# Feed-forward by seven block products for eight, in two phases, with half of the weight sums on GpSimd

## The reference

```
def swiglu_ffn(hn, w_gate, w_up, w_down):
    return (jax.nn.silu(hn @ w_gate) * (hn @ w_up)) @ w_down

h = h + swiglu_ffn(rms_norm(h, norm_ffn_w[l]), w_ffn_gate[l], w_ffn_up[l], w_ffn_down[l])
h = rms_norm(h, norm_final_w)
return h[:, N_META:]
```

## Time and profile before

| | |
|---|---|
| median of 3 runs | 2921.02 us (2920.89 to 2921.11) |
| span of the profiled execution | 2921.4 us |
| the profiled execution's own time | no figure apart from its span, which is 0.4 us above the median |
| PE busy | 2891.1 us, 14928 matmuls |
| DVE, ACT, POOL busy | 1146.6, 760.4, 354.5 us |
| moved | 280.75 MB, 96 GB/s on average |

### The profile page before, as it was taken

One profiled execution on the slowest core, in us unless ns is written; L12 is line 12 of the kernel. 1 busy time (PEld: TensorE's weight loads), 2 busy tenths in 40 slices (PEclk: granted clock), 3 DMA queues, 4 the chain that ended last, 5 costly groups with the idle time before them and its releaser, 6 DMA issues.

```text
span 2921.4 us, 38375 instructions
## 1 busy us (share of the span) xinstructions
PE 2891.1 (99%) x14928; PEld 2449.9 (84%) x14928; DVE 1146.6 (39%) x1436; ACT 760.4 (26%) x929; POOL 354.5 (12%) x358
## 2 busy tenths in 40 slices
PE   8999999999999999999999999999999999999998
PEld 8999888888889878888888888888888888888887
DVE  4444555555452344422432323333332323233334
ACT  4443322222222322222322222222222222222222
POOL 5000244433334201100200000000000000000000
PEclk9999999999999999999999999999999999999999
DMA  4333222222223324433133333232323233232322
GB/s 142 87 87 93 73 80 80 79 79 79 85 80 108 94 82 148 151 123 122 58 101 96 96 97 95 94 94 94 94 94 95 96 97 95 94 94 94 94 94 108
DMA packets 234900, 280.75 MB, mean 96 GB/s; under 512 B 10777, under 2 KB 192162, under 8 KB 234146
## 3 DMA queue, kind: packets, MB, share of 16 engines
q1 hardware_dynamic: 230450, 270.91, 29.7%
q10 hardware_dynamic: 4352, 8.39, 0.8%
HBM read 266.68 MB, written 12.58 MB: 96 GB/s over the span
## 4 chain that ended last, share of the span: by engine, by line
PE 97%; DVE 1%; ACT 1%; issue 1%; POOL 1%; DMA 0%; SPq 0%; DVEq 0%; POOLq 0%; ACTq 0%
PE psum L1395 66%; PE psum L1421 7%; PE psum L1420 7%; PE psum L1419 7%; PE psum L1577 2%; PE psum L1372 1%; PE psum L1572 1%; PE psum L1347 1%; PE psum L1556 0%; PE psum L1650 0%; POOL hn_lo L475 0%; PE psum L1534 0%; ACT f_junk L913 0%; PE psum L1550 0%; PE psum L1547 0%
## 5 line engine op out<-in xcount | busy, mean ns | idle before, releaser
L923 DVE TENSOR_TENSOR w_lo<-w_raw,w_hi 128x1024 fp32r<-128x1024 f32 x472 | 589.9, 1250 | 1301.9 <-ACT w_hi L653 1300.3
L1395 PE MATMUL psum<-hn_lo,w_hi 128*128 128x512 f32 (+1 forms) x2976 | 997.8, 361 | 0.0
L1395 PE MATMUL psum<-hn_hi,w_lo 128*128 128x512 f32 (+1 forms) x2976 | 994.4, 360 | 0.0
L1395 PE MATMUL psum<-hn_hi,w_hi 128*128 128x512 f32 (+1 forms) x2976 | 993.1, 360 | 0.0
L653 ACT ACTIVATE w_hi<-w_raw 128x1024 fp32r<-128x1024 f32 x472 | 499.5, 1058 | 1540.4 <-PE psum L1395 945.2
L1395 PEld LDWEIGHTS psum<-hn_hi,w_hi 128*128 128x128 f32 x2976 | 528.8, 188 | 85.1 <-issue 0.2
L1395 PEld LDWEIGHTS psum<-hn_lo,w_hi 128*128 128x128 f32 x2976 | 527.8, 188 | 84.3 <-issue 0.7
L1395 PEld LDWEIGHTS psum<-hn_hi,w_lo 128*128 128x128 f32 x2976 | 528.5, 188 | 81.3
L1420 PE MATMUL psum<-w_lo,a_hi 128*128 128x512 f32 x672 | 265.8, 396 | 0.0
L1421 PE MATMUL psum<-w_hi,a_lo 128*128 128x512 f32 x672 | 265.8, 395 | 0.0
L1419 PE MATMUL psum<-w_hi,a_hi 128*128 128x512 f32 x672 | 265.7, 395 | 0.0
(11 more groups left out here) (280 smaller groups left out, 2277.5 us busy)
## 6 DMA issues: line engine op xcount, KB each, us to landing
w_raw<-in_w_in SPq DMA_DIRECT2D x144, 512.0 KB, 3.6
w_raw<-in_w_ffn_gate SPq DMA_DIRECT2D x88, 512.0 KB, 3.5
w_raw<-in_w_ffn_up SPq DMA_DIRECT2D x88, 512.0 KB, 3.5
w_raw<-in_w_ffn_down SPq DMA_DIRECT2D x88, 512.0 KB, 3.7
w_raw<-in_w_out SPq DMA_DIRECT2D x32, 512.0 KB, 3.7
gates_dram<-gate_out ACTq DMA_DIRECT2D x16, 512.0 KB, 2.8
w_raw<-in_w_proj_a SPq DMA_DIRECT2D x16, 512.0 KB, 6.5
w_raw<-in_w_proj_b SPq DMA_DIRECT2D x16, 512.0 KB, 8.2
```

Of the source, the lines that this page charges most:

```text
L923: dve.tensor_tensor(wlo[s][:], raw[s][:], whi[s][:].bitcast(F32), ALU.subtract).then_inc(S["lo_ready"], 1)
L1395: ins = pe.matmul(o, lhs, r, start=kt == 0 and i == 0, stop=kt == 4 * n_chunks - 1 and i == 2)
```

## The change

The feed-forward is cut into blocks, and each 2x2 block product is formed with seven products of blocks instead of eight (Winograd's form of Strassen's scheme): some blocks are added first, and the results are combined with more additions. It is done in two phases: first gate and up for all 5632 hidden columns, with the activations written to a DRAM tensor, then down.

Gate and up. A unit is 256 columns of gate or of up: 22 pairs of units. The weights of a unit (2048x256, `fraw`, two buffers) are four blocks: upper and lower half of the rows, left and right 128 columns. The token side is split once, ahead: seven combinations of y = the normalised h (`s_hi`, `s_lo`), each 1024 rows by 256 tokens. A product is 24 matmuls over 256 columns. Per unit:
- VectorE forms two sums of weight blocks in one instruction (`t_pair`, `t13`: two times 1024 elements).
- GpSimd forms the other two (`sums`: `t2`, and then in place in `fraw`), 1024 elements each, the second after the first.
- ScalarE writes the high parts in four instructions (`hi_a`, `hi_2`, `hi_b`, `hi_c`: 2048, 1024, 2048, 2048 elements), VectorE the low parts (`low_a`, `low_2`, `low_b`, `low_c`). None of these buffers is doubled.
- Banks of PSUM are read in the middle of the sums: three copies on ScalarE (`e0`, `e1`, `e0`) and three additions on VectorE (C11, C22, C12; `c_done`).

Per pair ScalarE applies silu, VectorE multiplies and forms four sums (`up_products`), the seven results of 256 tokens (`comb`) are split and stored to DRAM by two transfers that ScalarE issues (`comb_store`, 0.92 MB each).

Down runs in twelve steps of 512 plus 512 columns: for each block of hidden rows (2, 4, 4, 4, 4, 4 times 256) two steps. Per step SyncE loads four blocks of weights, VectorE forms four sums of them (`dn_sum`), ScalarE and VectorE split seven blocks, and VectorE adds each of the seven products from PSUM to `hq`, which holds h in quarters (`dn_read`, 1024 elements). h is stored to DRAM during the output projection and read back as `hq`; y is written over h. Every second step the activations of the next block are loaded. The final norm comes after the last of these.

The core of the diff, with the instructions that the prediction speaks of:

```diff
-            gate_up(G_FFN, 0)
-            with sp.Fori(0, N_FFN // 2) as i:
-                g = G_FFN + 16 + 48 * i
-                gate_up(g, 2 * i + 1)
-                down(g + 16, 2 * i)
-                gate_up(g + 24, 2 * i + 2)
-                down(g + 40, 2 * i + 1)
-            down(G_END - 8, N_FFN - 1)
+            sp.wait_ge(S["lo_ready"], G_FFN)
+            ffn_load(0, 0)
+            sp.wait_ge(S["h1_ready"], FREE["h1_ready"] + TT * N_OUT)
+            store_h(N_OUT - 1)
+            sp.wait_ge(S["s_sum"], 4)
+            sp.wait_ge(S["x_lo"], X0 // 2 + 4)
+            ffn_load(0, 1)
+            with sp.Fori(1, PAIRS) as j:
+                for g in range(2):
+                    sp.wait_ge(S["lo_ready"], half_of(2 * j + g - 1, 3))
+                    ffn_load(j, g)
...
+            sp.wait_ge(S["comb_stored"], 32 * KAPPA[0])
+            for q, what in enumerate(ORDER):
+                sp.wait_ge(S["chunk_used"], USED0 + 7 * (UNITS - 1) + min(q // 2 + 1, 4))
+                act_load(0, what)
+            sp.wait_ge(S["chunk_used"], USED0 + 7 * UNITS - 2)
+            hq_load(0)
...
+            def sums(j, g):
+
+                n = 2 * j + g
+                pool.wait_ge(S["t_done"], n + 1)
+                after(pool, "chunk_used", 7 * n - 4, USED0)
+                pool.tensor_tensor(t2[:], t13[:, 0, :, :], fraw[g][:, HEADS:KT, P:UNIT], ALU.add).then_inc(S["t_pool"], 1)
+                pool.wait_ge(S["t_pool"], 2 * n + 1)
+                pool.tensor_tensor(fraw[g][:, 0:HEADS, P:UNIT], t2[:], fraw[g][:, HEADS:KT, 0:P], ALU.add) \
+                    .then_inc(S["t_pool"], 1)
...
+            def unit_act(j, g, last=False, beside=lambda: None):
+
+                n = 2 * j + g
+                act.wait_ge(S["chunk_used"], USED0 + 7 * n + 1)
+                after(act, "c_done", 3 * (n) - 1)
+                act.activation(e0[:], PS[:, 3 * g, 0:UNIT], ACT.Copy).then_inc(S["evicted"], 1)
+                split_c(n, g)
+                act.wait_ge(S["chunk_used"], USED0 + 7 * n + 3)
+                after(act, "c_done", 3 * (n) - 0)
+                act.activation(e1[:], PS[:, 3 * g, 0:UNIT], ACT.Copy).then_inc(S["evicted"], 1)
+                if not last:
+                    split_a(j + g, 1 - g)
+                act.wait_ge(S["chunk_used"], USED0 + 7 * n + 4)
+                act.wait_ge(S["c_done"], 3 * (n + 1) - 2)
+                act.activation(e0[:], PS[:, 3 * g + 2, 0:UNIT], ACT.Copy).then_inc(S["evicted"], 1)
+                beside()
+                if not last:
+                    split_2(n + 1)
+                    split_b(n + 1)
...
+            def pair_act(j, first=False, last=False):
+                def beside():
+                    if not first:
+                        comb_high(j - 1)
+
+                unit_act(j, 0, False, beside)
+                if not first:
+                    comb_store(j - 1)
+                silu(j)
+                unit_act(j, 1, last)
...
+            def unit_dve(j, g, last=False, begin=lambda: None, beside=lambda: None):
+
+                n = 2 * j + g
+                dst = (sg, comb)[g]
+                low_b(n)
+                begin()
+                if g == 1:
+                    after(dve, "comb_stored", 32 * j)
+                dve.wait_ge(S["chunk_used"], USED0 + 7 * n + 2)
+                dve.wait_ge(S["evicted"], 3 * (n + 1) - 2)
+                dve.tensor_tensor(dst[:, C_11, :], e0[:], PS[:, 3 * g + 1, 0:UNIT], ALU.add).then_inc(S["c_done"], 1)
+                low_c(n, g)
+                if not last:
+                    low_a(j + g, 1 - g)
+                beside()
+                dve.wait_ge(S["chunk_used"], USED0 + 7 * n + 5)
+                dve.wait_ge(S["evicted"], 3 * (n + 1) - 0)
+                dve.tensor_tensor(dst[:, C_22, :], e0[:], PS[:, 3 * g, 0:UNIT], ALU.subtract).then_inc(S["c_done"], 1)
+                if not last:
+                    t_pair(j + g, 1 - g)
+                dve.wait_ge(S["chunk_used"], USED0 + 7 * n + 6)
+                dve.wait_ge(S["evicted"], 3 * (n + 1) - 1)
+                dve.tensor_tensor(dst[:, C_12, :], PS[:, 3 * g + 2, 0:UNIT], e1[:], ALU.subtract).then_inc(S["c_done"], 1)
+                if not last:
+                    low_2(n + 1)
...
+            def low_2(n):
+                dve.wait_ge(S["hi_ready"], half_of(n + 1, 1))
+                dve.wait_ge(S["t_pool"], 2 * n + 2)
+                dve.tensor_tensor(lo_2[:], t2[:], hi_2[:].bitcast(F32), ALU.subtract).then_inc(S["lo_ready"], 1)
...
+            def unit_pe(j, g, first=False):
+
+                n = 2 * j + g
+                a, b, c = (PS[:, 3 * g + i, 0:UNIT] for i in range(3))
+                pe.wait_ge(S["lo_ready"], half_of(n + 1, 0))
+                after(pe, ("silu", "ay_done")[g], 2 * j)
+                product(A11, hi_a, lo_a, 0, a, True, False, first)
+                after(pe, "c_done", 3 * (n - 1) - 2)
+                product(A12, hi_a, lo_a, HEADS, b, True, True, first)
+                pe.wait_ge(S["lo_ready"], half_of(n + 1, 1))
+                pe.wait_ge(S["evicted"], 3 * (n + 1) - 2)
+                product(S2, hi_2, lo_2, 0, a, False, False, first)
+                pe.wait_ge(S["lo_ready"], half_of(n + 1, 2))
+                after(pe, "c_done", 3 * (n - 1) - 0)
+                product(S1, hi_b, lo_b, 0, c, True, False, first)
+                pe.wait_ge(S["evicted"], 3 * (n + 1) - 1)
+                product(S3, hi_b, lo_b, HEADS, a, False, False, first)
+                pe.wait_ge(S["lo_ready"], half_of(n + 1, 3))
+                pe.wait_ge(S["evicted"], 3 * (n + 1) - 0)
+                product(S4, hi_c, lo_c, HEADS, c, False, True, first)
+                pe.wait_ge(S["c_done"], 3 * (n + 1) - 1)
+                product(A22, hi_c, lo_c, 0, a, False, True, first)
```

More of the change, by code:

```diff
@@ L116 @@
[L116 to L120, removed]
+PAIRS = FFN // UNIT
+UNITS = 2 * PAIRS
+A11, A12, S2, S1, S3, S4, A22 = range(7)
+KAPPA = (2, 4, 4, 4, 4, 4)
+FIRST_PAIR = tuple(sum(KAPPA[:b]) for b in range(len(KAPPA)))
+DN_UNITS = 2 * len(KAPPA)
+ORDER = ("b11", "b21", "t2", "t1", "t3", "b22", "t4")
@@ new lines, in hybrid_block @@
+        fraw = [place(f"ffn_raw{i}", [P, KT, UNIT], at=raw_at[i]) for i in range(2)]
+        hi_a = place("hi_a", [P, KT, P], F32R, at=whi_at)
+        lo_a = place("lo_a", [P, KT, P], F32R, at=whi_at + 8192)
+        hi_b = place("hi_b", [P, KT, P], F32R, at=wlo_at)
+        hi_c = place("hi_c", [P, KT, P], F32R, at=wlo_at + 8192)
+        lo_c = place("lo_c", [P, KT, P], F32R, at=mixer_consts_at)
+        e0 = place("e0", [P, UNIT], at=mixer_consts_at + 8192)
+        e1 = place("e1", [P, UNIT], at=mixer_consts_at + 8192 + 1024)
@@ new lines, in hybrid_block @@
+        assert mixer_consts_at + 8192 + 2048 <= s_at
+        t13 = place("t13", [P, 2, HEADS, P], at=ext_at)
+        lo_b = place("lo_b", [P, KT, P], F32R, at=ext_at)
+        t2 = place("t2", [P, HEADS, P], at=ext_at + 8192)
+        lo_2 = place("lo_2", [P, HEADS, P], F32R, at=ext_at + 8192)
+        hi_2 = place("hi_2", [P, HEADS, P], F32R, at=ext_at + 12288)
+        comb = place("comb", [P, 7, UNIT], at=after_s + 16384)
+        comb_lo = place("comb_lo", [P, 7, UNIT], F32R, at=after_s + 16384)
@@ L906, in _ @@
[L906 to L914 removed]
+                if c < 4:
+                    split(G_OUT + 8 * (N_OUT - 1) + c + 4, c)
@@ new lines, in pair_dve @@
+            def pair_dve(j, first=False, last=False):
+                if first:
+                    unit_dve(j, 0, False, lambda: (s_low(S3, 9), s_low(S4, 10), dve.wait_ge(S["x_lo"], X0 // 2 + 6)))
+                else:
+                    unit_dve(j, 0, False, lambda: up_products(j - 1), lambda: comb_low(j - 1))
+                unit_dve(j, 1, last)
+            pair_dve(0, True)
+            with dve.Fori(1, PAIRS - 1) as j:
+                pair_dve(j)
+            pair_dve(PAIRS - 1, False, True)
@@ L1326, in _ @@
+            for q in range(4, 7):
+                dn_read(DN_UNITS - 1, q)
+            dve.wait_ge(S["rows_landed"], 96)
+            for t in range(TT):
+                dve.wait_ge(S["x_squared"], SQ_F + 8 + 4 * (t // 2) + (3 + t % 2))
+                dve.tensor_reduce(rms_s[:, t:t + 1], ssf[:, 4 * t:4 * t + 4], AX.X, ALU.add).then_inc(S["f_summed"], 1)
                 dve.wait_ge(S["f_summed"], t + 1)
```

666 lines of the change are left out of this document (463 added, 203 removed).

## The result

The changed kernel takes 2785.81 us (median of 4 runs, 2784.52 to 2786.37), the kernel before in the same session 2921.07 (4 runs, 2920.89 to 2921.79): a ratio of 0.9535 [0.9521, 0.9549], 135 us less. The prediction was 63 us less, with a range from 2810 to 2905. The span of the profiled execution is 2784.3 us.

The account below looks back on a forecast made before the run. Waits through VectorE, GpSimd and the store were taken to bound gate and up, at 42.0 us a pair against TensorE's 39.76. 1439.3 start + 37.3 unit 0 + 903 gate and up + 455 down + 18.7 tail + 5 clock = 2858 us, range 2810 to 2905.

Parts of the forecast that it names:

- the walk: Steady gate and up: instruction durations added link by link along the waits, giving 42.0 us a pair of units.
- the ring: Gate and up: waits running from unit to unit through single buffers, VectorE, GpSimd and the store, setting 42.0 us a pair.
- The gate half: First unit of a steady pair: bound by VectorE and GpSimd in series, 21.1 us against TensorE's 19.88.
- The up half: Second unit of a steady pair: C11 waits for the store of comb, 20.7 us, 20.9 with hand-offs.
- Rival 1: Gate and up: TensorE stays the bound, a pair takes 39.8 us, 47 us less, total 2811; chance 0.13.
- GpSimd and VectorE hindering each other: Shared SBUF port as an exclusive lock: at most 0.5 us a pair, but 8 us in the first unit.
- Unit 0: First unit of gate and up: 37.3 us, where a steady unit takes 21; TensorE stands some 9 us.
- Down: Down projection: 431 us of matmuls plus 24 of waits, 455 us; steps hidden behind TensorE from step 2 on.
- rival 3: Down: transfers bind; at 153 GB/s a step takes 51.4 us, total 2980 us; chance 0.08.
- Clock: TensorE's clock falls after it has stood: three falls charged, 1.7 us each time, 5 us.
- Rival 4: Gate and up: the clock falls in every pair, 37 us more, total 2895; chance 0.11.
- Rival 2: Gate and up: GpSimd's sums take some 4.4 us each, +8 us a pair, total 3030 us; chance 0.06.

Follow-up runs that it names:

- e2: Changed kernel with ScalarE waiting for hi_b's completion before it issues the stores of comb: 2818.27 us, ratio 0.9646 to the kernel before.
- e4: Kernel before, its eight products kept, with every 512-token gate and up matmul cut into two of 256 columns: 2930.6 us, ratio 1.0033 to the kernel before.
- e3: Changed kernel with one more GpSimd addition of 512 elements ahead of each unit's two sums: 2841.81 us, ratio 0.9726 to the kernel before.
- e6: Changed kernel with token tile 0 scaled after read 5 of down's last step and tile 1 after read 6: 2784.39 us, ratio 0.9529 to the kernel before.
- e10: Changed kernel with token tiles 0 and 1 both scaled between the last two reads of PSUM: 2780.97 us, ratio 0.9515 to the kernel before.

## Why the prediction was wrong, point by point

The step that failed is the wait that it put ahead of the store of comb: "The store stands in ScalarE's queue behind hi_2 and hi_b of the next unit", at 1.06 + 1.92 us. The store went out 0.49 us after the first GpSimd sum. With that put right, and the 1.3 us a pair by which the walk was too long, the ring of VectorE, GpSimd and the store is some 38.1 us (an estimate: 20.58 in the gate half of e2, and 18.43 less C22's 0.90 of idle time in the up half), under TensorE's 39.25, and TensorE sets the pair.

- **What bounds it, and the TensorE work.** Right in kind. The matmul counts are those of the page, and down's pitch is 233 ns. The pitch at 256 columns was 1.5 ns too high, 11 us over 7392 matmuls; it came from one pair of starts in the first half-unit. e4 confirms the lower one. The forecast itself did not use it, as it took the ring's 42.0.
- **The gate half,** predicted 21.1, is 20.82 in the changed kernel and 20.58 where nothing else holds it (e2). The walk by durations was 2.5% too long: instructions that follow each other on VectorE overlap by 0.09 us (lo_2 and lo_b start 1.14 apart, lo_2 lasts 1.23), and the hand-offs cost less than that gives back, where the prediction let the two cancel.
- **The up half failed** at one step, "the store stands in ScalarE's queue behind hi_2 and hi_b". It does by program order, but the issue doesn't wait for their execution: 2.5 us. e2 makes it wait, and the ring appears: 40.66 a pair with a TensorE stand in each. So this step turned a kernel that TensorE bounds (39.25) into one bound by a ring, and it is worth 1.41 us a pair, 30 us. The other 1.34 us a pair up to 42.0, 29 us, are the walk's excess in both halves. Together they are the 59 us of the table.
- **Rival 1** is what happened in the pairs, and it had a chance of only 0.13. Its condition was not met as written: the store took 7.0 us, not under 5.4, but began 2.5 us sooner. Its 2811 is still some 27 us above the span, by the pitch (11 us) and by the other terms of the table (15 us).
- **GpSimd and VectorE hindering each other.** Nothing in the steady pair (GpSimd's sums 2391 ns on average), as argued. The 0.5 us a pair that the prediction charges is not in its 42.0 either, and its unit 0 adds up to 37.1 by its own terms, for the 37.3 written. In the first unit it shows as one VectorE sum of 4.46 us where 2.29 is normal, beside GpSimd's split of y:

```profile
1445.99 4.46 DVE L1551 TENSOR_TENSOR s_sum<-s_sum,h 128x2048 f32<-128x2048 f32 x1
```
```profile
1445.71 6.95 POOL L774 TENSOR_TENSOR s_lo<-h,s_hi 128x1024 fp32r<-128x1024 f32 x2 [9.65 <-ACT s_hi L1101]
```
```profile
1448.26 4.40 POOL L774 TENSOR_TENSOR s_lo<-h,s_hi 128x1024 fp32r<-128x1024 f32 x1
```

  The second line is two GpSimd splits, 2.59 us and then the 4.40 of the third line. The two engines take turns: GpSimd's first split ends at 1448.30, VectorE's sum 2.15 later (1450.45), GpSimd's second split 2.21 after that (1452.66), and VectorE's next split, of 4.32 us, 2.15 after that (1454.81). The three long instructions last 4.3 to 4.5 us because each record begins while the other engine is still at work. The rule of the Trainium skill (SBUF — State Buffer, "SBUF: two separate sides"), that the shared port pair is held for a whole instruction, agrees with these rows. On VectorE two such, 2.2 and 2.0 us longer, and a lo_a of 3.27 make 5.2 of the 8 charged. The lock had no weight in the steady pair, as GpSimd works there while VectorE stands.
- **Unit 0,** 33.65 for 37.3: hindrance of 4.2 us after the first product for some 7, and back-to-back instructions overlap by up to 0.09 us each. The stand after two products is 8.4 us for "some 9".
- **Down.** 449.9 for 455. The stand after the first two products, predicted 11, is 7.25, released by `hq` as foreseen:

```profile
2330.60 0.77 PE L2119 MATMUL psum<-dn_hi,act_hl 128*128 128x512 f32 x1 [7.25 <-DVE hq L1662]
```

  Transfers run at 201 GB/s and a share of 0.60 over the stage (201 and 0.63 predicted), so rival 3 is out: the 176 GB/s of the earlier trace rows was demand, not a limit.
- **Tail.** 18.2 for 18.7, by the same four scalings.
- **Clock.** Where the window means are under one (0.77 in unit 0, 0.88 and 0.90 at the start of down) it falls to its lower level for a part of the window, around stands of TensorE: a mean of 0.53 from 1450 to 1461 beside the stand of 8.4 us, 0.57 from 2327 to 2335 beside that of 7.25, 0.57 from 2368 to 2376 beside one of 3.1. In all the steady units it is 1.00. Rival 4 is out, and not only because TensorE never stands there: in e2 and e3 it stands 1.15 and 1.64 us in a pair, and the mean from 1500 to 2280 is 1.00 in both. The charge of 5 us was a term of its own, but it is in the measured stages.
- **Rival 2** (GpSimd at its worst rows) is out: 2391 ns. e3 shows that its reasoning was sound. With 0.34 us of slack, 1.37 us more a unit cost 56 us.

## What to carry to other kernels

On ScalarE here, an instruction that only issues a transfer waits for semaphores, its own and those of the work ahead of it, but not for the end of that work. Where a trace of before has such an issue, read its own time there, and don't add the durations ahead of it. Where a walk of a ring ends within some 6% of another engine's time, as 42.0 and 39.76 do, the two cases deserve like chances, and each ring has to be walked through every engine that it crosses, the busy one too. An instruction moved into an engine's idle time gains only if nobody waits for what is queued behind it (e6 against e10).

## What the runs showed of the hardware that was not expected

- ScalarE's queue issued a transfer 0.06 us before the activation that precedes it in the program had begun (1827.52 and 1827.58), and 1.96 us before that activation's end. The median over the first 21 pairs is the same 0.06.
- GpSimd and VectorE, both with two inputs in SBUF, took turns by whole instructions (ends at 1448.30, 1450.45, 1452.66 and 1454.81), and the time waited stands inside the record of the one that waits (4.46 us for 2.29, 4.40 for 2.39).
- The DMA engines moved 381 GB/s over 28 us. In the steady units the share of 0.47 goes with 152 GB/s.
- Matmuls of 256 columns have a pitch of 116.8 to 116.9 ns, 0.504 of that of 512, with a weight load for each (PE and PEld both x17736).
